# First mixer of a three-layer block on one core: heads one after another, division folded into the norm

## The chip, the cores and the metric

The kernel runs on one core of a Trainium2 chip, as one launch. The metric is the device time in microseconds (us). TensorE is called PE, VectorE DVE, ScalarE ACT, GpSimd POOL, SyncE SP, as in the profile.

## The reference, cut to what matters

Three layers with residual stream `x` of 512 tokens by 1024 features, fp32. The first layer's mixer is an mLSTM with 4 heads (keys 128 wide, values 256 wide). Per chunk it computes:

```python
d = jnp.exp(log_d - m_t[..., None])
s = jnp.einsum('bhtd,bhsd->bhts', qb, kb) * d
...
den = jnp.sum(s, axis=-1) + inter * jnp.einsum('bhd,bhtd->bht', n, qb)
h_out = num / jnp.maximum(jnp.abs(den), jnp.exp(-m_t))[..., None]
...
hs = rms_norm(hs, head_gain.reshape(H, dv))
og = jax.nn.sigmoid(o.astype(jnp.float32)).reshape(B, S, H, dv)
out = (hs * og).reshape(B, S, D_MODEL).astype(h.dtype)
return out @ w_out
```

After it come a residual add with a norm, cross-attention into 256 memory tokens, a feed-forward part, and two more layers, which the change leaves alone.

## The kernel before

Features lie on the partitions and the 512 tokens along the free dimension. The kernel computes the chunked recurrence as one causal attention over all 512 tokens: per head a score matrix in four blocks of 512, 384, 256 and 128 columns (1280 in all, offsets `AT`), times a decay matrix `ml_w`. Weights come from memory in units of 128x1024 (8 tiles of 128x128): SP loads a unit into one of 2 landing buffers, ACT writes its upper half `w_hi` (L777, `hi_to`), POOL the rest `w_lo` (L1731, `lo_to`), both into a ring of 4. A tile of a projection is three matmuls (`tile`, L359): upper by upper, upper weights by lower activations, lower weights by upper activations; so an output of 8 tiles is 24 matmuls of 512 columns. The mixer's inner products (scores, sums, values) are plain fp32 matmuls. A unit's ring place comes free when PE has multiplied it (`unit_done`). All five engines run their own list of instructions in order, tied by semaphores; `await_empty` makes PE wait until a PSUM bank was read out.

Order of the first mixer: projections q, k, the gates, the output gate `ml_og` (DVE L1228, ACT sigmoid), then the values `ml_v` by token (`by_token`, L416: two groups of four units, banks 0 to 3, then 4 to 7). Then PE spreads two rows per head over all partitions (L457), one for the decays (`M_bc`, copied by DVE L1311), one for the denominator's floor (`floor_bc`, ACT L890), and turns `uT` (L461). DVE computes the decays' arguments (L1323), ACT their exponentials (L895).

Then the heads go in two pairs. For a pair: both heads' scores (PE L470), both heads' weights and causal mask (DVE L1331, L1335), then for each head the sum over the weights (denominator, 1280 columns) and two value products (numerator, 2560 columns; both PE L481). ACT takes the denominator's absolute value (L901), DVE its maximum with the floor (L1343), its reciprocal (L1345) and the product with the numerator out of PSUM (L1350). ACT squares the result (L905), PE sums the squares over partitions (L492, L493), ACT computes the reciprocal root (L907, L909); POOL multiplies by the output gate (L1778) meanwhile. DVE applies root (L1357) and gain (L1359), ACT writes the upper half `u_hi` (L913), DVE the lower half `u_lo` (L1363). The second pair's arguments and weights begin on DVE after the first pair's `u_lo`. The projection `ml_out` (L359) waits for all eight `u_lo` tiles, then makes its 8 outputs one after another; ACT copies each out (L821), DVE sums squares (L1250, L1252), and the memory's norm is computed beside it (L928, L1372).

Of the kernel before, what the change touches and what calls it, by code (L numbers as in the profile page):

```python
# [14 lines left out]
P = 128  # L15
# [135 lines left out]
def build(nc, units, xT, memT, vecs_d, gates_w, gates_b, pool_w, conv_d, consts_d, masks_d, out):  # L151
    assert units.shape[0] == UNITS
    ctx = ExitStack()
    with ctx:
# [109 lines left out]
        for name, size in (("e0", 1024), ("e1", 1024), ("a0", 1024), ("a1", 1024), ("sc", 1024), ("state", 512),  # L264
# [27 lines left out]
        ml_og_at, ml_arg, ml_exp, ml_s, ml_den, ml_h_at, ml_sq, ml_r, ml_gated, ml_scaled = (  # L292
            sem(n) for n in ("ml_og", "ml_args", "ml_decays", "ml_weights", "ml_den", "ml_h", "ml_h_squared", "ml_h_rstd", "ml_h_gated", "ml_h_scaled"))
# [48 lines left out]
        def tensor_engine():  # L342
# [92 lines left out]
            def mlstm():  # L435
# [13 lines left out]
                by_token("ml_v", u_tok, 4)  # L449
                for h in range(ML_H):  # L450
                    sel = sel_all[0:4, h * P:(h + 1) * P]
                    b = 2 * (h % 2)
                    for bank, row in ((b, w1), (b + 1, w2)):
                        if h == 0:
                            pe.wait_ge(*(ml_gate_v.at(7) if bank == 0 else ml_gate_s.at(7)))
                        await_empty([bank])
                        pe.matmul(ps[:, bank, :], sel, row, start=True, stop=True).then_inc(*full[bank].up())  # L457
                        holds(("ml_bc", h, bank % 2), [bank], full[bank].now())
                await_empty([0])
                for b in range(4):  # L460
                    ins = pe.transpose(ps[:, 0, 4 * b:4 * b + 4], rows[0:4, 0, b * P:(b + 1) * P], ident[0:4, 0:4])  # L461
                ins.then_inc(*full[0].up())
                holds("ml_uT", [0], full[0].now())
                for i in range(2):
                    for j in range(2):
                        h, B0 = 2 * i + j, 3 * j
                        await_empty([B0, B0 + 1, B0 + 2])
                        for b in range(4):
                            a0 = 512 * B0 + AT[b]
                            ins = pe.matmul(flat[:, a0:a0 + S - b * P], ml_kT[:, h, b * P:(b + 1) * P], ml_qT[:, h, b * P:S],  # L470
                                            start=b != 3, stop=b != 1, skip_group_check=True)
                        ins.then_inc(*full[B0].up())
                        holds(("ml_s", h), [B0, B0 + 1, B0 + 2], full[B0].now())
                    for j in range(2):
                        h, B0 = 2 * i + j, 3 * j
                        for n in range(3):
                            if n == 0:
                                pe.wait_ge(*ml_s.at(h + 1))
                            for b in range(4):
                                lhs = ones if n == 0 else ml_v[:, b, h * ML_DV + (n - 1) * P:h * ML_DV + n * P]  # L480
                                ins = pe.matmul(ps[:, B0 + n, b * P:S], lhs, ml_w[:, j, AT[b]:AT[b] + S - b * P],  # L481
                                                start=b == 0, stop=b == 3, skip_group_check=True)
                            if n == 0:
                                ins.then_inc(*full[B0].up())
                                holds(("ml_den", h), [B0], full[B0].now())
                        ins.then_inc(*full[B0 + 1].up())
                        holds(("ml_num", h), [B0 + 1, B0 + 2], full[B0 + 1].now())
                    for j in range(2):
                        h = 2 * i + j
                        pe.wait_ge(*ml_sq.at(h + 1))  # L490
                        await_empty([6 + j])
                        pe.matmul(ps[:, 6 + j, :], ones, sq[:, 0, 0:S], start=True, stop=False)  # L492
                        pe.matmul(ps[:, 6 + j, :], ones, sq[:, 1, 0:S], start=False, stop=True).then_inc(*full[6 + j].up())  # L493
                        holds(("ml_ss", h), [6 + j], full[6 + j].now())
                pe.wait_ge(*o_lo_at.at(8))
                outputs("ml_out", SQUARE, u_rhs, ONE, four)
# [270 lines left out]
        def scalar_engine():  # L767
# [65 lines left out]
            def mlstm():  # L833
# [35 lines left out]
                table("natural_log_exp_and_others")  # L869
                for j in range(8):  # L870
# [6 lines left out]
                    if j == 1:  # L877
                        act.wait_ge(*ml_gate_s.now())
                        act.activation(w1, w1, ACT.Ln, bias=1.0).then_inc(*ml_gate_s.up())
                    if j % 4 == 3:  # L880
# [4 lines left out]
                    if j == 4:  # L885
                        act.wait_ge(*ml_gate_v.at(9))
                        act.activation(w2, w2, ACT.Exp, scale=-1.0).then_inc(*ml_gate_s.up())
                for h in range(ML_H):
                    act.wait_ge(*ready_at["ml_bc", h, 1])
                    act.activation(floor_bc[:, h, :], ps[:, banks_at["ml_bc", h, 1][0], :], ACT.Copy).then_inc(*emptied_by["ml_bc", h, 1])  # L890
                for i in range(2):
                    for j in range(2):
                        h = 2 * i + j
                        act.wait_ge(*ml_arg.at(h + 1))
                        act.activation(ml_w[:, j, :], ml_w[:, j, :], ACT.Exp, scale=-1.0).then_inc(*ml_exp.up())  # L895
                    for j in range(2):
                        h, B0 = 2 * i + j, 3 * j
                        act.wait_ge(*ready_at["ml_den", h])
                        if i:
                            act.wait_ge(*o_lo_at.at(2 * h - 2))  # L900
# [5 lines left out]
                        act.wait_ge(*ready_at["ml_ss", h])  # L906
# [287 lines left out]
        def vector_engine():  # L1194
            def own():

                dve.wait_ge(*dve_own.now())
# [714 lines left out]
```

## Time and profile before

| | |
|---|---|
| time, 3 runs | median 2699.49 us (2697.83 to 2703.25) |
| profiled execution: its time | 2702.27 us |
| its span | 2700.9 us |
| PE matmul busy | 2456.8 us (91%) |
| DVE / ACT / POOL busy | 982.2 / 897.1 / 1064.4 us |
| mean granted TensorE clock | 0.951 |

Times in views are us from the start of the span. A matmul's end is modelled, so consecutive matmuls overlap in the list; the chain of waits gives better durations for a run of them. A granted clock of 1.00 is 2.4 GHz, 0.50 is 1.2 GHz.

### The profile page before, as it was taken

To read this page: it belongs to the slowest core of one execution; us is meant where nothing else is said; L and a number is where in the kernel's file an instruction comes from. 1 tells how busy PE (TensorE), PEld (TensorE's weight loads), DVE (VectorE), ACT (ScalarE), POOL (GpSimd) and SP (SyncE) were. 2 spreads that over 40 slices of the span, in tenths; PEclk is the share of its full clock that TensorE was granted. 3 is DMA by queue.
4 is the path that set the end of the run, shared out by engine and by line. 5 is a ranking of instruction groups with operands and counts; after the bars stand their busy time and mean duration, and the time that the engine had idled before them with its cause. 6 is when DMAs were issued, how large, how long until landed. Compare 5 with 4: busy or idle time off the path is not lost.

```text
span 2700.9 us, 29218 instructions
## 1 busy us (share of the span) xinstructions
PE 2456.8 (91%) x12268; PEld 2017.8 (75%) x12268; DVE 982.2 (36%) x1312; ACT 897.1 (33%) x1194; POOL 1064.4 (39%) x466
## 2 busy tenths in 40 slices
PE   7986898899999798989888999997998998899997
PEld 5754775678888586668666788885988998799885
DVE  3245623422211411444423422204556442754402
ACT  4322432332222323664323322223434323322221
POOL 5321551444444442005514444444423433444442
PEclk9987998899999898999899999998989999999998
DMA  4211230122233121003312222222200222132231
GB/s 146 86 39 34 99 125 24 56 101 97 98 101 102 63 94 55 1 1 102 125 39 70 71 94 97 99 102 85 87 32 27 99 79 79 63 99 91 92 109 70
DMA packets 62850, 211.47 MB, mean 78 GB/s; under 512 B 8704, under 2 KB 10880, under 8 KB 62720
## 3 DMA queue, kind: packets, MB, share of 16 engines
q1 hardware_dynamic: 57968, 206.20, 22.8%
q10 hardware_dynamic: 4752, 3.42, 0.4%
q8 instruction: 97, 1.59, 0.2%
q14 instruction: 33, 0.27, 0.0%
HBM read 207.49 MB, written 2.10 MB: 78 GB/s over the span
## 4 chain that ended last, share of the span: by engine, by line
PE 80%; DVE 12%; ACT 4%; issue 2%; DMA 1%; POOL 0%; ACTq 0%; SPq 0%; DVEq 0%
PE ps L359 64%; PE ps L416 4%; DVE x L1212 3%; DVE u_lo L1203 2%; DVE arena L1210 2%; PE ps L544 1%; PE ps L611 1%; PE ps L651 1%; PE ps L524 1%; PE ps L481 1%; DVE y_ffn L1210 1%; PE ps L597 1%; PE ps L587 1%; PE ps L599 1%; DMA w_land<-in_units 1%
## 5 line engine op out<-in xcount | busy, mean ns | idle before, releaser
L1731 POOL TENSOR_TENSOR w_lo<-w_land,w_hi 128x1024 fp32r<-128x1024 f32 x384 | 955.1, 2489 | 1398.6 <-ACT w_hi L777 1398.2
L359 PE MATMUL ps<-u_hi,w_hi 128*128 128x512 f32 (+2 forms) x2448 | 800.1, 358 | 99.5 <-DVE u_lo L1203 62.6
L359 PE MATMUL ps<-u_lo,w_hi 128*128 128x512 f32 (+2 forms) x2448 | 797.1, 357 | 0.0
L359 PE MATMUL ps<-u_hi,w_lo 128*128 128x512 f32 (+2 forms) x2448 | 792.8, 355 | 0.0
L359 PEld LDWEIGHTS ps<-u_hi,w_hi 128*128 128x128 f32 x2448 | 437.5, 191 | 188.5 <-issue 51.5
L777 ACT ACTIVATE w_hi<-w_land 128x1024 fp32r<-128x1024 f32 x384 | 403.2, 1051 | 478.8 <-PE ps L359 350.4
L359 PEld LDWEIGHTS ps<-u_hi,w_lo 128*128 128x128 f32 x2448 | 435.3, 191 | 66.4
L359 PEld LDWEIGHTS ps<-u_lo,w_hi 128*128 128x128 f32 x2448 | 434.9, 191 | 66.0 <-issue 0.7
L359 PE MATMUL ps<-hid_hi,w_lo 128*128 128x512 f32 x528 | 208.3, 395 | 0.0
L359 PE MATMUL ps<-hid_lo,w_hi 128*128 128x512 f32 x528 | 208.3, 395 | 0.0
L359 PE MATMUL ps<-hid_hi,w_hi 128*128 128x512 f32 x528 | 208.3, 395 | 0.0
L1250 DVE TENSOR_TENSOR sq<-y_ffn 128x512 f32<-128x512 f32 x24 | 16.6, 692 | 329.7 <-ACT y_ffn L821 329.7
L1228 DVE TENSOR_TENSOR arena<-ps,rstd 128x264 f32<-128x264 f32 (+1 forms) x92 | 46.0, 530 | 247.0 <-PE ps L359 230.2
L1463 DVE TENSOR_TENSOR arena<-ps,rstd 128x512 f32<-128x512 f32 x66 | 45.6, 690 | 239.3 <-PE ps L359 239.3
L999 ACT ACTIVATE hid_hi<-arena 128x512 fp32r<-128x512 f32 x66 | 41.7, 631 | 246.6 <-DVE arena L1466 246.6
L359 PEld LDWEIGHTS ps<-hid_hi,w_lo 128*128 128x128 f32 x528 | 99.5, 188 | 23.3
L359 PEld LDWEIGHTS ps<-hid_hi,w_hi 128*128 128x128 f32 x528 | 99.5, 188 | 23.2
L359 PEld LDWEIGHTS ps<-hid_lo,w_hi 128*128 128x128 f32 x528 | 99.5, 188 | 23.1
L1740 POOL TENSOR_TENSOR acc<-acc,sq 128x512 f32<-128x512 f32 (+1 forms) x42 | 66.0, 1571 | 57.5 <-ACT sq L800 56.6
L1250 DVE TENSOR_TENSOR sq<-arena 128x512 f32<-128x512 f32 (+1 forms) x40 | 27.8, 695 | 163.4 <-ACT arena L821 163.4
L796 ACT ACTIVATE u_hi<-x,vecs 128x512 fp32r<-128x512 f32 (+1 forms) x64 | 46.3, 723 | 120.5 <-DVE x L1212 120.5
L821 ACT ACTIVATE arena<-ps 128x512 f32<-128x512 f32 (+1 forms) x48 | 24.5, 529 | 160.2 <-PE ps L359 160.2
(281 smaller groups left out, 2930.0 us busy)
## 6 DMA issues: line engine op xcount, KB each, us to landing
w_land<-in_units SPq DMA_DIRECT2D x384, 512.0 KB, 3.2
x<-in_xT SPq DMA_DIRECT2D x4, 528.0 KB, 7.1
arena<-in_memT ACTq DMA_DIRECT2D x2, 1024.0 KB, 5.2
outT<-x SPq DMA_DIRECT2D x8, 256.0 KB, 2.0
consts<-in_consts SPq DMA_DIRECT2D x1, 448.0 KB, 7.8
arena<-in_masks ACTq DMA_DIRECT2D x1, 448.0 KB, 3.4
arena<-in_consts ACTq DMA_DIRECT2D x1, 296.0 KB, 3.8
arena<-in_consts ACTq DMA_DIRECT2D x1, 256.0 KB
```

The costliest lines, as they stand in the source:

```text
L359: ins = pe.matmul(ps[:, bank, 0:c1 - c0], w, rhs(k, c0, c1)[which], start=first and h == 0, stop=last and h == 2)
L416: ins = pe.matmul(ps[:, 4 * g + b, :], a_, w_[:, u % RING, cols], start=k == 0 and n == 0, stop=k == DT - 1 and n == 2)
L777: act.activation(w_hi[:, u % RING, :], w_land[:, u % LAND, :], ACT.Copy).then_inc(*unit_hi.up())
L796: act.activation(u_hi[:, k, a:z], x[:, k, a:z], ACT.Copy, scale=col(gain, k)).then_inc(*u_hi_at.up())
L1203: dve.scalar_tensor_tensor(u_lo[:, k, a:z], x[:, k, a:z], col(gain, k), u_hi[:, k, a:z].bitcast(F32), ALU.mult, ALU.subtract).then_inc(*u_ ...
L1210: dve.scalar_tensor_tensor(y[:, k, :], y[:, k, :], col(POST[p], k), rstd_y[:, cols], ALU.mult, ALU.mult).then_inc(*dve_own.up())
L1212: dve.tensor_tensor(x[:, k, cols], x[:, k, cols], y[:, k, :], ALU.add).then_inc(*x_new.up())
L1228: ins = dve.tensor_tensor(v, p_, rstd[:, c0:c1], ALU.mult)
L1250: dve.tensor_tensor(sq[:, o % 2, 0:w], y[:, o, :], y[:, o, :], ALU.mult).then_inc(*dve_own.up())
L1463: dve.tensor_tensor(w, bank, rs, ALU.mult).then_inc(*emptied_by[name, o])
L1731: pool.tensor_tensor(w_lo[:, u % RING, :], w_land[:, u % LAND, :], w_hi[:, u % RING, :].bitcast(F32), ALU.subtract).then_inc(*unit_lo.up())
L1740: pool.tensor_tensor(acc[:, a:z], acc[:, a:z], sq[:, k % 2, a:z], ALU.add).then_inc(*x_sum.up())
```

## The change

- The heads go one by one. The next head's scores are issued behind this head's denominator and ahead of the previous head's sum of squares and this head's numerator. Each engine's list is rewritten to match: while head h's weights, denominator and numerator are made, head h-1 is normed.
- The spreading of the rows (8 matmuls and `uT`) moves between units 5 and 6 of `ml_v`; the copies, the arguments and the exponentials of heads 0 and 1 move with it on DVE and ACT. The ACT copies of the floor become squares.
- Division folded into the norm: ACT squares denominator and numerator straight out of PSUM (scaled by eps for the denominator); DVE adds the floored square to the mean square; ACT's reciprocal root of that serves for both. Reciprocal, product and absolute value go.
- The output gate is multiplied by DVE out of PSUM; POOL's four gate products go. Root and gain are one instruction per tile.
- `ml_out` begins its first three outputs abreast, tile by tile as each `u_lo` comes; the other five follow as before.

```diff
-    by_token("ml_v", u_tok, 4)
...
+    def broadcasts():
+
+        for h in range(ML_H):
...
+                pe.matmul(ps[:, bank, :], sel, row, start=True, stop=True).then_inc(*full[bank].up())
...
+    by_token("ml_v", u_tok, 4, [(5, broadcasts)])
...
+    def weighted(h, n, lhs):
+        B0 = 3 * (h % 2)
...
+            ins = pe.matmul(ps[:, B0 + n, b * P:S], lhs(b), ml_w[:, h % 2, AT[b]:AT[b] + S - b * P],
...
+    def denominator(h):
+        B0 = 3 * (h % 2)
+        pe.wait_ge(*ml_s.at(h + 1))
+        weighted(h, 0, lambda b: ones).then_inc(*full[B0].up())
...
+    def numerator(h):
+        B0 = 3 * (h % 2)
+        for n in range(2):
+            ins = weighted(h, n + 1, lambda b: ml_v[:, b, h * ML_DV + n * P:h * ML_DV + (n + 1) * P])
+        ins.then_inc(*full[B0 + 1].up())
...
+    def square_sum(h):
+        bank = 6 + h % 2
+        pe.wait_ge(*ml_sq.at(h + 1))
+        await_empty([bank])
+        pe.matmul(ps[:, bank, :], ones, sq[:, 0, 0:S], start=True, stop=False)
+        pe.matmul(ps[:, bank, :], ones, sq[:, 1, 0:S], start=False, stop=True).then_inc(*full[bank].up())
...
+    scores(0)
+    scores(1)
     for h in range(ML_H):
...
-            ins.then_inc(*full[B0].up())
...
-                    pe.wait_ge(*ml_s.at(h + 1))
...
-                    ins = pe.matmul(ps[:, B0 + n, b * P:S], lhs, ml_w[:, j, AT[b]:AT[b] + S - b * P],
...
-            pe.wait_ge(*ml_sq.at(h + 1))
...
-            pe.matmul(ps[:, 6 + j, :], ones, sq[:, 0, 0:S], start=True, stop=False)
-            pe.matmul(ps[:, 6 + j, :], ones, sq[:, 1, 0:S], start=False, stop=True).then_inc(*full[6 + j].up())
...
-    pe.wait_ge(*o_lo_at.at(8))
-    outputs("ml_out", SQUARE, u_rhs, ONE, four)
+        denominator(h)
+        if 1 <= h < ML_H - 1:
+            scores(h + 1)
+        if h:
+            square_sum(h - 1)
+        numerator(h)
+    square_sum(ML_H - 1)
+
+    for o in range(3):
+        await_empty(four(o))
+    for k in range(UT):
+        pe.wait_ge(*o_lo_at.at(k + 1))
+        for o in range(3):
+            ins = tile(UNIT["ml_out"] + o, k, k, u_rhs, ONE, four(o), k == 0, k == UT - 1)
+            if k == UT - 1:
+                ins.then_inc(*unit_done.up())
+                holds(("ml_out", o), four(o), unit_done.at(UNIT["ml_out"] + o + 1))
+    outputs("ml_out", SQUARE, u_rhs, ONE, four, 3)
...
+        if j == 6:
+            for h in range(ML_H):
+                act.wait_ge(*ready_at["ml_bc", h, 1])
+                act.activation(floor_bc[:, h, :], ps[:, banks_at["ml_bc", h, 1][0], :], ACT.Square, scale=EPS ** 0.5).then_inc(*emptied_by["ml_bc", h, 1])
+            decays(0)
+            decays(1)
...
+    def denominator_square(h):
+
...
+        if h >= 2:
+            act.wait_ge(*ml_scaled.at(2 * h - 2))
+        act.activation(d, ps[:, 3 * (h % 2), :], ACT.Square, scale=EPS ** 0.5).then_inc(*emptied_by["ml_den", h])
...
+    def numerator_square(h):
+        act.wait_ge(*ready_at["ml_num", h])
+        if h:
+            act.wait_ge(*ready_at["ml_ss", h - 1])
+        act.activation(sq[:, :, 0:S], ps[:, 3 * (h % 2) + 1:3 * (h % 2) + 3, :], ACT.Square).then_inc(*ml_sq.up())
...
+    def rstd_head(h):
+        d = den[h % 2]
+        act.wait_ge(*emptied_at["ml_ss", h])
+        act.activation(d, d, ACT.Ln).then_inc(*act_own.up())
+        act.wait_ge(*act_own.now())
+        act.activation(d, d, ACT.Exp, scale=-0.5).then_inc(*ml_r.up())
...
+    def uppers(h):
+        for n in range(2):
+            kk = 2 * h + n
+            act.wait_ge(*ml_scaled.at(kk + 1))
+            act.activation(u_hi[:, kk, XS], ml_h[:, 2 * (h % 2) + n, :], ACT.Copy).then_inc(*o_hi_at.up())
...
     for h in range(ML_H):
...
-            act.activation(den[j], ps[:, B0, :], ACT.Abs).then_inc(*emptied_by["ml_den", h])
-            act.wait_ge(*emptied_at["ml_num", h])
-            if h:
-                act.wait_ge(*ready_at["ml_ss", h - 1])
-            act.activation(sq[:, :, 0:S], ml_h[:, 2 * j:2 * j + 2, :], ACT.Square).then_inc(*ml_sq.up())
...
-            act.activation(den[j], ps[:, 6 + j, :], ACT.Ln, bias=eps[:, 0:1], scale=1.0 / ML_DV).then_inc(*emptied_by["ml_ss", h])
-            act.wait_ge(*emptied_at["ml_ss", h])
-            act.activation(den[j], den[j], ACT.Exp, scale=-0.5).then_inc(*ml_r.up())
...
+        denominator_square(h)
+        if h:
+            rstd_head(h - 1)
+            uppers(h - 1)
+        numerator_square(h)
+        if h + 2 < ML_H:
+            decays(h + 2)
+    rstd_head(ML_H - 1)
+    uppers(ML_H - 1)
...
+        if j == 6:
+            for h in range(ML_H):
+                dve.wait_ge(*ready_at["ml_bc", h, 0])
+                dve.tensor_copy(M_bc[:, h, :], ps[:, banks_at["ml_bc", h, 0][0], :]).then_inc(*emptied_by["ml_bc", h, 0])
+            dve.wait_ge(*ready_at["ml_uT"])
...
+            arguments(0)
+            arguments(1)
...
+    def weights(h):
...
+        dve.tensor_tensor(w, flat[:, 512 * 3 * (h % 2):512 * 3 * (h % 2) + SPAN], w, ALU.mult).then_inc(*emptied_by["ml_s", h])
...
+    def floor(h):
...
+        dve.tensor_tensor(den[h % 2], den[h % 2], floor_bc[:, h, :], ALU.max).then_inc(*dve_own.up())
+
+    def gated(h):
+        B0, n = 3 * (h % 2), 2 * (h % 2)
+        dve.wait_ge(*ready_at["ml_num", h])
...
+        dve.wait_ge(*ml_sq.at(h + 1))
...
+        dve.tensor_tensor(ml_h[:, n:n + 2, :], ps[:, B0 + 1:B0 + 3, :], ml_og[:, 2 * h:2 * h + 2, :], ALU.mult).then_inc(*emptied_by["ml_num", h])
+
+    def mean_square(h):
...
+        dve.wait_ge(*ready_at["ml_ss", h])
...
+        dve.scalar_tensor_tensor(d, ps[:, 6 + h % 2, :], 1.0 / ML_DV, d, ALU.mult, ALU.add).then_inc(*emptied_by["ml_ss", h])
+
+    def normed(h):
+        dve.wait_ge(*ml_r.at(h + 1))
...
+        for n in range(2):
+            h_ = ml_h[:, 2 * (h % 2) + n, :]
+            dve.scalar_tensor_tensor(h_, h_, col("ml_head", 2 * h + n), den[h % 2], ALU.mult, ALU.mult).then_inc(*ml_scaled.up())
...
+    weights(0)
+    weights(1)
     for h in range(ML_H):
...
-            dve.tensor_tensor(den[j], den[j], floor_bc[:, h, :], ALU.max).then_inc(*dve_own.up())
...
-            dve.reciprocal(den[j], den[j]).then_inc(*dve_own.up())
...
-            dve.tensor_tensor(h_, ps[:, B0 + 1:B0 + 3, :], one(den[j]).broadcast_to([P, 2, S]), ALU.mult).then_inc(*emptied_by["ml_num", h])
...
-                dve.tensor_tensor(h_, h_, one(den[n // 2]).broadcast_to([P, 2, S]), ALU.mult).then_inc(*dve_own.up())
...
-            dve.tensor_scalar(ml_h[:, n, :], ml_h[:, n, :], col("ml_head", kk), None, ALU.mult).then_inc(*ml_scaled.up())
...
+        floor(h)
+        if 1 <= h < ML_H - 1:
+            weights(h + 1)
+        if h:
+            mean_square(h - 1)
+            normed(h - 1)
+            lowers(h - 1)
+        gated(h)
+        if h + 2 < ML_H:
+            arguments(h + 2)
+    mean_square(ML_H - 1)
+    normed(ML_H - 1)
+    lowers(ML_H - 1)
...
-pool.wait_ge(*ml_og_at.at(8))
-for h in range(ML_H):
-    j = h % 2
-    h_ = ml_h[:, 2 * j:2 * j + 2, :]
-    pool.wait_ge(*ml_sq.at(h + 1))
-    pool.tensor_tensor(h_, h_, ml_og[:, 2 * h:2 * h + 2, :], ALU.mult).then_inc(*ml_gated.up())
```

## Rows read from the trace of the kernel before

**Rows 1.** The profile's page: busy shares, and the chain's shares by engine.

```profile
PE 2456.8 (91%) x12268; PEld 2017.8 (75%) x12268; DVE 982.2 (36%) x1312; ACT 897.1 (33%) x1194; POOL 1064.4 (39%) x466
...
PE 80%; DVE 12%; ACT 4%; issue 2%; DMA 1%; POOL 0%; ACTq 0%; SPq 0%; DVEq 0%
```

**Rows 2.** Windows: length, busy time (instructions) by engine, granted clock, DMA share, GB/s.

```profile
160.40:169.90 9.50, 9.26 (x21) 3.93 (x20) 4.26 (x7) 3.58 (x6) 0.00 (x0) 0.77 0.08 32
177.20:192.10 14.90, 14.88 (x54) 8.80 (x52) 7.66 (x8) 1.65 (x2) 2.35 (x1) 1.00 0.00 0
192.10:200.50 8.40, 0.04 (x1) 0.04 (x1) 6.41 (x5) 2.86 (x4) 0.01 (x1) 0.74 0.00 0
209.70:216.30 6.60, 0.01 (x2) 0.01 (x1) 6.57 (x15) 2.54 (x2) 0.00 (x0) 0.77 0.00 0
233.10:241.50 8.40, 0.03 (x1) 0.03 (x1) 6.41 (x5) 2.86 (x4) 0.00 (x1) 0.74 0.00 0
241.50:251.30 9.80, 3.78 (x5) 1.17 (x5) 7.55 (x10) 3.51 (x6) 2.34 (x1) 0.50 0.00 0
```

**Rows 3.** The chain of waits from 100 to 300: start, length, what.

```profile
115.88 44.53 PE ps L416 x192
160.41 8.92 PE ps L457 x16
...
177.35 13.01 PE ps L481 x48
190.36 0.86 PE ps L492 x2
...
235.72 3.36 DVE rstd_y L1345
...
251.27 40.53 PE ps L359 x168
```

**Rows 4.** A window over a stretch in which the granted clock stood at 0.50.

```profile
165.46:175.70 10.24, 9.97 (x19) 4.91 (x18) 5.85 (x12) 3.73 (x4) 0.00 (x0) 0.50 0.00 0
```

**Rows 5.** Groups by line, 160.4 to 251.3: busy us, mean ns | idle before, releaser.

```profile
L1323 DVE SCALAR_TENSOR_TENSOR arena<-arena,uT,zrow 128x512 f32<-128x512 f32 (+3 forms) x16 | 7.6, 545 | 0.0
...
L1331 DVE TENSOR_TENSOR arena<-ps,arena 128x1280 f32<-128x1280 f32 x4 | 5.9, 1487 | 1.3 <-PE ps L470 1.3
...
L895 ACT ACTIVATE arena<-arena 128x1280 f32<-128x1280 f32 x4 | 5.1, 1270 | 6.6 <-DVE arena L1323 6.6
...
L913 ACT ACTIVATE u_hi<-arena 128x512 fp32r<-128x512 f32 x8 | 4.6, 617 | 1.5 <-DVE arena L1359 1.5
L905 ACT ACTIVATE sq<-arena 128x1024 f32<-128x1024 f32 x4 | 4.2, 1057 | 21.6 <-DVE arena L1350 21.6
L1335 DVE TENSOR_TENSOR arena<-arena,consts 128x128 f32<-128x128 f32 x16 | 3.6, 285 | 0.1
...
L1357 DVE TENSOR_TENSOR arena<-arena,rstd_y 128x1024 f32<-128x1024 f32 x2 | 2.5, 1225 | 4.3 <-ACT rstd_y L909 4.3
L1350 DVE TENSOR_TENSOR arena<-ps,acc 128x1024 f32<-128x1024 f32 x2 | 2.4, 1224 | 0.1
...
L1343 DVE TENSOR_TENSOR rstd_y<-rstd_y,arena 128x512 f32<-128x512 f32 x2 | 1.4, 692 | 16.8 <-ACT rstd_y L901 16.8
L907 ACT ACTIVATE acc<-ps,eps 128x512 f32<-128x512 f32 x2 | 1.4, 687 | 10.9 <-PE ps L493 10.9
...
L909 ACT ACTIVATE rstd_y<-rstd_y 128x512 f32<-128x512 f32 x2 | 1.3, 630 | 0.1
```

**Rows 6.** Timeline of DVE, 306 to 330: a two-factor product of 512 columns.

```profile
308.54 0.74 DVE L1210 SCALAR_TENSOR_TENSOR arena<-arena,vecs,rstd_y 128x512 f32<-128x512 f32 x1
```

**Rows 7.** Timeline of ACT, 251 to 310: the third output's copy.

```profile
269.58 0.60 ACT L821 ACTIVATE arena<-ps 128x512 f32<-128x512 f32 x1 [4.01 <-PE ps L359]
```

**Rows 8.** The page's groups: the making of a unit's two halves.

```profile
L1731 POOL TENSOR_TENSOR w_lo<-w_land,w_hi 128x1024 fp32r<-128x1024 f32 x384 | 955.1, 2489 | 1398.6 <-ACT w_hi L777 1398.2
...
L777 ACT ACTIVATE w_hi<-w_land 128x1024 fp32r<-128x1024 f32 x384 | 403.2, 1051 | 478.8 <-PE ps L359 350.4
```

More of the change, by code:

```diff
@@ L448, in mlstm @@
                 outputs("ml_og", SQUARE, u_rhs, ONE, four)
-                by_token("ml_v", u_tok, 4)
-                for h in range(ML_H):
[L451 to L458, printed above, removed]
@@ L495, in mlstm @@
-                pe.wait_ge(*o_lo_at.at(8))
-                outputs("ml_out", SQUARE, u_rhs, ONE, four)
+                def broadcasts():
+                    for h in range(ML_H):
+                        sel = sel_all[0:4, h * P:(h + 1) * P]
+                        b = 2 * (h % 2)
+                        for bank, row in ((b, w1), (b + 1, w2)):
+                            if h == 0:
+                                pe.wait_ge(*(ml_gate_v.at(7) if bank == 0 else ml_gate_s.at(7)))
+                            await_empty([bank])
+                            pe.matmul(ps[:, bank, :], sel, row, start=True, stop=True).then_inc(*full[bank].up())
+                            holds(("ml_bc", h, bank % 2), [bank], full[bank].now())
+                    await_empty([0])
+                    for b in range(4):
+                        ins = pe.transpose(ps[:, 0, 4 * b:4 * b + 4], rows[0:4, 0, b * P:(b + 1) * P], ident[0:4, 0:4])
+                    ins.then_inc(*full[0].up())
+                    holds("ml_uT", [0], full[0].now())
@@ new lines, in mlstm, with scores @@
+                by_token("ml_v", u_tok, 4, [(5, broadcasts)])
+                def scores(h):
+                    B0 = 3 * (h % 2)
+                    await_empty([B0, B0 + 1, B0 + 2])
+                    for b in range(4):
+                        a0 = 512 * B0 + AT[b]
+                        ins = pe.matmul(flat[:, a0:a0 + S - b * P], ml_kT[:, h, b * P:(b + 1) * P], ml_qT[:, h, b * P:S],
+                                        start=b != 3, stop=b != 1, skip_group_check=True)
+                    ins.then_inc(*full[B0].up())
+                    holds(("ml_s", h), [B0, B0 + 1, B0 + 2], full[B0].now())
@@ new lines, in weighted @@
+                def weighted(h, n, lhs):
+                    B0 = 3 * (h % 2)
+                    for b in range(4):
+                        ins = pe.matmul(ps[:, B0 + n, b * P:S], lhs(b), ml_w[:, h % 2, AT[b]:AT[b] + S - b * P],
+                                        start=b == 0, stop=b == 3, skip_group_check=True)
+                    return ins
+                def denominator(h):
+                    B0 = 3 * (h % 2)
+                    pe.wait_ge(*ml_s.at(h + 1))
+                    weighted(h, 0, lambda b: ones).then_inc(*full[B0].up())
+                    holds(("ml_den", h), [B0], full[B0].now())
@@ L869, in mlstm, with decays @@
                 table("natural_log_exp_and_others")
+                def decays(h):
+                    act.wait_ge(*ml_arg.at(h + 1))
+                    act.activation(ml_w[:, h % 2, :], ml_w[:, h % 2, :], ACT.Exp, scale=-1.0).then_inc(*ml_exp.up())
                 for j in range(8):
@@ L879, in mlstm @@
                         act.activation(w1, w1, ACT.Ln, bias=1.0).then_inc(*ml_gate_s.up())
+                    if j == 4:
+                        act.wait_ge(*ml_gate_v.at(9))
+                        act.activation(w2, w2, ACT.Exp, scale=-1.0).then_inc(*ml_gate_s.up())
+                    if j == 6:
[4 more added lines that the diff above has]
+                        decays(1)
                     if j % 4 == 3:
@@ new lines, in rstd_head @@
+                def rstd_head(h):
+                    d = den[h % 2]
+                    act.wait_ge(*emptied_at["ml_ss", h])
[7 more added lines that the diff above has]
+                        act.activation(u_hi[:, kk, XS], ml_h[:, 2 * (h % 2) + n, :], ACT.Copy).then_inc(*o_hi_at.up())
```

140 lines of the change are left out of this document (39 added, 101 removed).

## Prediction

> **What bounds the kernel now.** I read the page first. PE is busy for 91% of the span and makes up 80% of the chain that ended last, DVE 12%, ACT 4% [rows 1]. So PE sets the time, and what can be won is time in which PE stands still or runs slowly. The page's average says nothing of the stretch that the change touches, so I cut that stretch into windows between the events of the chain. Here the reader sees the picture turn: PE is fully busy from 177.2 to 192.1, then has no work at all for 8.4 us, again for 6.6 us (209.7 to 216.3), again for 8.4 us (233.1 to 241.5), and from 241.5 to 251.3 works 3.78 of 9.8 us [rows 2]. That is 29.4 us of PE idle between the first denominator (177.35) and `ml_out` (251.27). In the gaps DVE is the busy one, and the chain of waits names its reciprocal with 3.36 us, one in each of the two 8.4 us gaps [rows 3]. The granted clock also falls: it stands at 0.50 in the last window of rows 2, and around the row spreading of L457 it is at 1.2 GHz for 10.24 us with PE busy for 9.97 of it, which is 5.1 us of work lost [rows 4].
>
> **Up to the first denominator.** A unit of `ml_v` takes 44.53/8 = 5.57 us, so unit 5 ends at 115.88 + 6 x 5.57 = 149.3 [rows 3]. Now the spreading comes in there: 8 matmuls at 0.86 (the price of one 512-column fp32 matmul, L492 in rows 3) and some 0.2 for `uT`, 7.1 us at 2.4 GHz. Then units 6 and 7, 11.1 us. The clock fell during the spreading before, which had full-rate work ahead of it as it has now, so I carry the loss of 5.1 us over [rows 4]; its bounds are nothing (no fall) and 7 us. `ml_v` ends at 149.3 + 7.1 + 11.1 + 5.1 = 172.6. What moves along costs nothing while this cover stands: copies, arguments (1.90 us per head, 7.6/4) and exponentials (1.27 us) of heads 0 and 1 [rows 5] are done by about 165 on idle engines, with some 8 us to spare. Queued behind ACT's wait for the arguments is the upper half of the third `ml_out` unit, wanted only 50 us later, and behind DVE's the value copies, which PE wants from the numerator on. Without the cover it would be the 4 to 5 us between spreading and scores that they cost before.
>
> Then head 0's scores. A head's 1280 columns take 13.01/6 = 2.17 us [rows 3]: 174.8. DVE's weights take 1.49 + 0.90 (3.6/4, mask) [rows 5], with 0.2 us from PE's last matmul to the consumer: 177.4. Before, the denominator began at 177.35 [rows 3]. So this move alone earns nothing: PE does the same work in another order, and loses the same to the clock.
>
> **The heads.** Denominator and numerator of head 0 are 3 x 2.17 = 6.5 us: 183.9. ACT squares the numerator (1.06, L905's price), DVE gates it (1.22, L1350's): 186.5. From there to the next head's gating a chain runs between DVE and ACT; in order, with the nearest row for each [rows 5, 6]: next but one head's arguments 1.90; exponentials 1.27; square of the denominator 0.60 (a 512-column ACT read of PSUM, rows 7); floor 0.69; weights 1.49 + 0.90; mean square 0.69 (as the floor; at most 0.74); Ln 0.69; Exp 0.63; two normed tiles 2 x 0.74; second upper half 0.62; square of the numerator 1.06; gating 1.22. That is 13.24, and 13.6 with twelve hand-overs of 0.03 us. PE's work in such a period is scores 2.17, denominator 2.17, sum of squares 1.72, numerator 4.34, together 10.4; it waits about 3.2 us for PSUM banks 3 to 5, which the gating empties. So DVE and ACT set the pace of the heads. Two periods: gating of head 2 ends at 213.7, having begun at 212.4.
>
> From 212.4 PE sets it again: sum of squares of head 2 1.72, numerator of head 3 4.34, 0.2, its square 1.06, its sum of squares 1.72, hand-overs 0.1: 221.5. Check by PE's account. Its work from 177.4 is 4 x 6.5 + 2 x 2.17 + 4 x 1.72 = 37.2 us in both kernels. Before, 73.9 us passed: 37.2 work, 29.4 idle, 7.3 lost to the clock. After, 44.1 us: 37.2 and 6.9 idle. The gain is 22.5 us of idle time and 7.3 us of clock.
>
> Operations with no row: squares out of two PSUM banks cost 1.06 (from SBUF) to 1.20 (two reads of 0.60), four on the path, so up to 0.6 us more; a gain is excluded, as no read here was cheaper by the column. The gating reads PSUM beside SBUF; rows show 1224 ns for that and 1225 ns with both factors in SBUF [rows 5], so no difference. The Trainium skill, VectorE: DVE Perf Modes, The TRN2 errata, gives a PSUM source 62 more cycles than an SBUF source; as an estimate that would be 65 ns a gating, 0.3 us in all. The trace does not agree, and the row stands.
>
> POOL's four products (L1778) vanish. Nothing on the path waited for them except in the order of DVE's scaling, and POOL is idle around them, so 0 us of their own; that DVE no longer meets POOL there is inside the prices above, which are those of quiet stretches.
>
> **`ml_out`.** PE has the tiles of heads 0 to 2 when it arrives at 221.5. Six tiles for three outputs are 12.5 us of work; the last tile needs 0.2 + 0.69 + 0.69 + 0.63 + 1.48 + 0.62 + 0.69 = 5.0 us after the last sum of squares, so it is hidden. Three outputs take 3 x 5.57 = 16.7 us: 238.2. The clock is at 2.4 GHz here if the waits before it are as short as worked out. Before, the third output was copied at 269.58 [rows 7], hence done at 269.4. After this the order is the old one. Three ring places come free almost together; the next unit but one needs a copy 0.60, upper half 1.05, lower half 2.49 [rows 7, 8], 4.1 us, beside a unit of 5.57. The cover is 1.4 us; if it were gone, each unit would be late by the excess. The memory's load is issued 17 us before the fourth output wants it.
>
> **The sum.** 269.4 - 238.2 = 31.2 us less. The profiled execution took 2702.3, 2.8 above the median of the runs; 2702.3 - 31.2 = 2671.1, by the median 2668.3.
>
> **Rivals.** (A) This forecast, 2664 to 2671 (small terms above, and falls of the clock in later stages landing elsewhere by a few us): 0.56.
>
> (B) The clock falls again in a 3.2 us wait between the heads. For: it fell within each gap of 6.6 us and more. Against: by the mean clocks 0.74 and 0.77 of those windows it was low for the last 4.4 of 8.4 us and the last 3.0 of 6.6 us, so it fell 3.6 to 4.0 us into them, later than a wait of 3.2 us lasts [rows 2]. One fall as long as in rows 4 costs at most 5.1 us, less what the wait absorbs: 2 to 5 us a fall, one or two falls, 2670 to 2678. Chance 0.25.
>
> (C) The spreading, being split from the scores by two dense units, costs little clock: up to 5 us more gain, 2660 to 2664. Chance 0.09.
>
> (D) The overlap fails: a wait, say of DVE in `normed` in front of the next gating, strings the heads up one by one and only reciprocals and products out of the way count. Two reciprocals and their products in the two gaps, 2 x (3.36 + 1.22) = 9.2 us: about 2690. Against: each order was followed above. Chance 0.06.
>
> (E) Slower: the clock goes down at the spreading and stays down, since PE now has a short wait in every head instead of a few long ones. PE's work from 156.4 to `ml_out` is 11.1 + 8.7 + 26.0 + 6.9 = 52.7 us; at 1.2 GHz 105.4, and three outputs 33.4: 295.2, 26 us later than before, 2725. It decides from some 62 us of low clock beyond the forecast. For it: low stretches outlast their cause by several us [rows 4]. Against: 2.4 GHz came back before 177 while PE ran the same kind of matmul. Chance 0.04. The Trainium skill, TensorE: Matmul & The Clock Gate, A second HAM failure mode, reports this kind of swing from small stops between groups of matmuls; by that rule B and E are the cases to fear, and no row of this trace shows it for stops this short.
>
> **How the numbers follow.** The likeliest case gives 2668. C and the later stages reach down to 2661, B up to 2676; D, E and the far end of B stay outside, about 1.5 in 10. What this kernel's measurement can tell from no change is about 0.2%, 5.4 us; A to D, 0.96, are faster by more; I leave 0.01 of it for no change and say faster 0.95, same 0.01, slower 0.04.
>
> **What would show it.** In the profile after: L1345, L1357, L1778 gone; `ml_v` ends near 172.6 and the first denominator starts near 177.4; gatings of heads 0, 1, 2 are 13.6 us apart, with PE stops of 3.2 us before the scores of head 3; the last sum of squares ends near 221.5 at granted clock 1.00; the third output is copied near 238. The prediction is wrong if DVE's or ACT's order adds a wait to the period, if the clock reads 0.50 between 180 and 221, or if PE waits for w_lo behind the third output.

## The result, and the profile after

The changed kernel takes 2674.94 us (median of 4 runs, 2673.47 to 2676.97) against 2701.37 us before on the same chip (4 runs, 2697.83 to 2703.28): ratio 0.9904 [0.9887, 0.9921], 26.4 us less. The forecast was 2668, its range 2661 to 2676. The profiled execution took 2673.47 us beside the 2702.27 us of before, 28.8 less where the sum said 31.2. Its mean granted clock is 0.960 (before 0.951).

The page's busy shares and chain by engine, after (before: [rows 1]):

```profile
PE 2446.1 (92%) x12268; PEld 2008.9 (75%) x12268; DVE 979.4 (37%) x1308; ACT 896.9 (34%) x1194; POOL 1055.9 (40%) x462
...
PE 77%; DVE 14%; ACT 5%; issue 2%; DMA 1%; POOL 1%; ACTq 0%; SPq 0%; DVEq 0%
```

PE issues the same 12268 matmuls, busy for 10.7 us less: that is clock. About half of it, 5.0 us, lies behind the first mixer, in stages that the change leaves alone. The rest of the gain is idle time. The chain of waits after, to be read against [rows 3]:

```profile
150.05 11.14 PE ps L459 x16
161.19 0.33 PE ps L463 x4
161.51 13.58 PE ps L416 x48
175.09 2.17 PE ps L474 x8
...
179.84 6.75 PE ps L482 x24
...
221.03 1.12 PE ps L503 x2
222.16 0.86 PE ps L504 x2
223.01 15.31 PE ps L359 x66
```

From the first denominator (179.84) to `ml_out` (223.01) is 43.2 us, where before it was 73.9. Windows over the same stretch, columns as in [rows 2]:

```profile
150.10:161.20 11.10, 11.10 (x19) 4.33 (x19) 2.77 (x4) 2.85 (x4) 2.34 (x1) 0.62 0.20 70
161.20:175.10 13.90, 13.90 (x52) 11.25 (x53) 3.96 (x9) 4.20 (x4) 2.39 (x1) 0.81 0.06 17
...
179.80:188.90 9.10, 8.90 (x32) 5.53 (x32) 4.15 (x8) 1.62 (x2) 0.00 (x0) 1.00 0.00 0
188.90:201.90 13.00, 10.59 (x36) 6.29 (x36) 9.46 (x18) 5.19 (x7) 0.00 (x0) 1.00 0.00 0
201.90:214.90 13.00, 11.87 (x39) 6.96 (x40) 9.46 (x18) 5.67 (x8) 0.00 (x0) 1.00 0.01 1
214.90:223.00 8.10, 6.99 (x23) 3.90 (x22) 5.27 (x7) 3.54 (x5) 0.00 (x0) 1.00 0.00 0
```

Here the reader sees both halves of the gain. The heads hold 4.85 us of idle PE (0.20 + 2.41 + 1.13 + 1.11) where [rows 2] had 29.4, and the clock reads 1.00 throughout. But in the first two windows, the row spreading and the two units behind it, PE is never idle and still runs at 0.62 and 0.81.

What became of the gain is read by marks, before against after: third output done 269.4 / 239.8 (29.6 us earlier); keys of the memory begin 298.23 / 270.37 (27.9); first scaling of `y`, the mixer's output, 305.43 / 278.24 (27.2, called **the mark** below, and in the expectations "DVE's first addition to x"); end of the span 2700.9 / 2672.2 (28.7). So 2.4 us are lost again between the third output and the mark, and 1.5 come back later: behind the mark PE is busy for 5.0 us less and idle for 3.6 us more. DVE's timeline after the third output shows the loss:

```profile
238.97 0.69 DVE L1304 TENSOR_TENSOR sq<-arena 128x512 f32<-128x512 f32 x1 [10.51 <-ACT arena L852]
239.70 0.69 DVE L1306 TENSOR_TENSOR acc<-acc,sq 128x512 f32<-128x512 f32 x1
240.48 2.73 DVE L1304 TENSOR_TENSOR sq<-arena 128x512 f32<-128x512 f32 x1
243.25 2.79 DVE L1306 TENSOR_TENSOR acc<-acc,sq 128x512 f32<-128x512 f32 x1
246.07 0.69 DVE L1304 TENSOR_TENSOR sq<-arena 128x512 f32<-128x512 f32 x1
```

and POOL's in the same microseconds, with PE's first matmul on the memory's keys:

```profile
239.97 5.51 POOL L1812 TENSOR_TENSOR w_lo<-w_land,w_hi 128x1024 fp32r<-128x1024 f32 x2 [7.99 <-ACT w_hi L808]
```

```profile
270.37 0.39 PE L359 MATMUL ps<-m_hi,w_hi 128*128 128x256 f32 x1 [2.44 <-DVE m_lo L1453]
```

The outputs that finish together hand DVE their sums in one bunch, while POOL makes two `w_lo` in one go. A sum that takes 0.69 us alone takes 2.73 and 2.79 when it begins while POOL's `w_lo` runs, DVE falls behind, and PE waits 2.44 us for `m_lo`, the lower half of the normed memory; before, that wait was 0.44. From the third output to the keys the chain of waits is DVE's alone; before, it was PE's there (L359 in [rows 3]) but for the last 6.4 us:

```profile
240.48 2.75 DVE sq L1304
...
243.25 2.80 DVE acc L1306
...
251.48 2.52 DVE m_lo L1453
...
265.47 2.82 DVE sq L1304
...
270.31 2.81 DVE sq L1304
```
The Trainium skill, SBUF — State Buffer, Who interferes with whom, says that a DVE instruction with two SBUF inputs contends with a GpSimd instruction that reads SBUF, and calls the contention an exclusive lock. DVE's and POOL's rows agree: the two slow sums take about as long as one `w_lo` (two in 5.51 us), while the sum at 239.70, begun 0.27 us ahead of POOL, takes 0.69. It is POOL that is then held up: in the kernel before, a `w_lo` that began 0.27 us behind such a sum took 2.69 us, where one that met no sum took 2.38.

### The profile page after: what moved, and what is told of

The parts are those of the page before. It is cut to its first block, busy times and chain, and to the rows that moved or that the text cites. A ratio compares the mean times of both kernels' runs of the same rounds, so it can differ in the third digit from the quotient of the medians.

```text
span 2672.2 us, 29212 instructions
## 1 busy us (share of the span) xinstructions
PE 2446.1 (92%) x12268; PEld 2008.9 (75%) x12268; DVE 979.4 (37%) x1308; ACT 896.9 (34%) x1194; POOL 1055.9 (40%) x462
## 4 chain that ended last, share of the span: by engine, by line
PE 77%; DVE 14%; ACT 5%; issue 2%; DMA 1%; POOL 1%; ACTq 0%; SPq 0%; DVEq 0%
PE ps L359 63%; PE ps L416 4%; DVE x L1266 3%; DVE u_lo L1257 2%; DVE arena L1264 2%; PE ps L575 1%; PE ps L642 1%; PE ps L555 1%; DVE y_ffn L1264 1%; DMA w_land<-in_units 1%; PE ps L618 1%; PE ps L682 1%; DVE sq L1304 1%; PE ps L628 1%; POOL w_lo L1812 1%
## 5 line engine op out<-in xcount | busy, mean ns | idle before, releaser
L359 PE MATMUL ps<-u_hi,w_hi 128*128 128x512 f32 (+2 forms) x2448 | 800.3, 358 | 95.6 <-DVE u_lo L1257 63.9
L359 PE MATMUL ps<-u_lo,w_hi 128*128 128x512 f32 (+2 forms) x2448 | 796.9, 357 | 0.0
L359 PE MATMUL ps<-u_hi,w_lo 128*128 128x512 f32 (+2 forms) x2448 | 793.4, 355 | 0.0
L359 PEld LDWEIGHTS ps<-u_hi,w_hi 128*128 128x128 f32 x2448 | 438.0, 191 | 183.7 <-issue 53.5
L359 PEld LDWEIGHTS ps<-u_hi,w_lo 128*128 128x128 f32 x2448 | 435.5, 191 | 66.1
L359 PEld LDWEIGHTS ps<-u_lo,w_hi 128*128 128x128 f32 x2448 | 435.4, 191 | 66.1 <-issue 1.0
L359 PE MATMUL ps<-hid_hi,w_lo 128*128 128x512 f32 x528 | 208.3, 395 | 0.0
L359 PE MATMUL ps<-hid_lo,w_hi 128*128 128x512 f32 x528 | 208.3, 395 | 0.0
L359 PE MATMUL ps<-hid_hi,w_hi 128*128 128x512 f32 x528 | 208.3, 394 | 0.0
L1544 DVE TENSOR_TENSOR arena<-ps,rstd 128x512 f32<-128x512 f32 x66 | 45.6, 691 | 239.8 <-PE ps L359 239.8
L359 PEld LDWEIGHTS ps<-hid_hi,w_hi 128*128 128x128 f32 x528 | 99.5, 188 | 23.4
L359 PEld LDWEIGHTS ps<-hid_hi,w_lo 128*128 128x128 f32 x528 | 99.5, 188 | 23.3
L359 PEld LDWEIGHTS ps<-hid_lo,w_hi 128*128 128x128 f32 x528 | 99.5, 188 | 23.0
L1304 DVE TENSOR_TENSOR sq<-arena 128x512 f32<-128x512 f32 (+1 forms) x40 | 37.4, 934 | 147.8 <-ACT arena L852 147.6
L1528 DVE TENSOR_TENSOR arena<-ps,rstd 128x512 f32<-128x512 f32 x44 | 30.4, 691 | 126.4 <-PE ps L359 104.6
```

The costliest lines, as they stand in the source:

```text
L359: ins = pe.matmul(ps[:, bank, 0:c1 - c0], w, rhs(k, c0, c1)[which], start=first and h == 0, stop=last and h == 2)
L1304: dve.tensor_tensor(sq[:, o % 2, 0:w], y[:, o, :], y[:, o, :], ALU.mult).then_inc(*dve_own.up())
L1544: dve.tensor_tensor(w, bank, rs, ALU.mult).then_inc(*emptied_by[name, o])
```

## The experiments

Each median is of 4 runs (6 for pairs_folded and order_alone). The mark is read from each profile; it resolves what the median cannot, since the time from the mark to the end of the span differed from profile to profile by up to 8.7 us (2390.8 to 2399.5) though nothing is changed there, and by 3.5 us between the three profiles of the changed kernel.

| label | median, us | ratio to before [95%] | mark, us |
|---|---|---|---|
| after_again | 2674.27 | 0.9886 [0.9869, 0.9902] | 278.38 |
| one_by_one | 2669.96 | 0.9865 [0.9850, 0.9880] | 273.76 |
| spread_late | 2671.99 | 0.9871 [0.9856, 0.9885] | 279.00 |
| spread_split | 2674.29 | 0.9882 [0.9867, 0.9897] | 275.90 |
| pairs_folded | 2693.67 | 0.9968 [0.9955, 0.9981] | 298.15 |
| order_alone | 2681.44 | 0.9923 [0.9909, 0.9937] | 288.14 |
| rows128 | 2669.05 | 0.9880 [0.9864, 0.9895] | 273.68 |
| split3_one | 2665.48 | 0.9870 [0.9856, 0.9884] | 273.70 |
| after_base | 2674.73 | 0.9905 [0.9884, 0.9927] | 278.45 |
| rows128_one | 2665.49 | 0.9870 [0.9850, 0.9889] | 271.45 |
| square_first | 2663.33 | 0.9857 [0.9836, 0.9878] | 268.58 |

Before stood at 2706.24 beside the first four, 2701.14 beside the next four, 2701.11 beside the last three; each of these three batches ran on another chip.

### The changed kernel again

> The changed kernel once more, as the base on the same chip for the three below: about 2675 us, 26 below the kernel before. Both theories expect the same: spreading at 1.2 GHz for 10 to 14 us, gatings about 13 us apart, PE 2.4 us idle before the keys of the memory.

> The changed kernel as the base on the same chip for the two below: 2673 to 2676 us, DVE's first addition to x near 278.5.

2674.27 and 2674.73 us: the same kernel, twice more. The PE stop of 2.44 us before the keys is there both times, and in none of the three profiles does the clock fall between the heads. The kernel before moved by 5 us from one batch to another, so differences to it are 26 to 32 us; kernels of one batch are compared with each other. The middle batch has no run of the changed kernel, so its four are compared with it by the marks and by the time before.

### Outputs one by one again

```diff
-for o in range(3):
-    await_empty(four(o))
-for k in range(UT):
-    pe.wait_ge(*o_lo_at.at(k + 1))
-    for o in range(3):
...
-outputs("ml_out", SQUARE, u_rhs, ONE, four, 3)
+output("ml_out", 0, SQUARE, u_rhs, ONE, four(0), {k: o_lo_at.at(k + 1) for k in range(UT)})
+outputs("ml_out", SQUARE, u_rhs, ONE, four, 1)
```

> Only edit: ml_out makes its first output alone, waiting tile by tile for the lower halves, instead of three abreast. Theory (the bunching costs): DVE's sums for the outputs no longer fall beside POOL's making of w_lo, PE's stop before the memory's keys goes back from 2.4 to about 0.4 us, the sum of y is ready about 0.7 us earlier, and the first output loses 0.8 us waiting for its last tiles: 1.5 to 2.5 us faster than three abreast. Rival (three abreast is worth its cover): the last tiles come 5 us after the last sum of squares and one output has only 4.1 us of work before them, so PE waits and the time is 1 us or more slower.

4.3 us faster than after_again, more than the 1.5 to 2.5 expected; the mark is 4.6 us earlier. DVE's sums of the third output, with 4.03 us of rest ahead of them, and PE's stop before the keys:

```profile
238.62 0.69 DVE L1296 TENSOR_TENSOR sq<-arena 128x512 f32<-128x512 f32 x1 [4.03 <-ACT arena L844]
239.34 0.69 DVE L1298 TENSOR_TENSOR acc<-acc,sq 128x512 f32<-128x512 f32 x1
```

```profile
266.56 0.39 PE L359 MATMUL ps<-m_hi,w_hi 128*128 128x256 f32 x1 [0.44 <-DVE m_lo L1445]
```

The bunch is gone and so is the stop; DVE still meets POOL in the first output's sums (2.52 and 2.77 us), but has caught up by the third. The last sum of squares ended 2.3 us earlier than in after_again (220.81 for 223.11), ahead of the edit and no effect of it: in this execution `ml_v` began 1.2 us earlier and the low clock of the spreading was shorter (10.2 us for 13.7), so `ml_v` ended at 172.43, though the clock fell again at head 3's scores:

```profile
199.40 3.78 PE L474 MATMUL ps<-arena 128*128 128x512 f32 x8 [2.38 <-DVE arena L1400]
```

The same scores take 2.39 us in the changed kernel. The other 2.3 us of the mark lie behind the last sum of squares and are the edit's, 2.0 of them the stop. The other profiles repeat it: from the last sum of squares to the mark it is 55.1 to 55.3 us in the six profiles of head-by-head kernels with three outputs abreast and the division folded, and 53.0 us in one_by_one, split3_one and rows128_one. So taking the outputs abreast costs here, and earns nothing.

### Where the spreading stands

Spread_late puts it back behind the eight units of `ml_v`; spread_split issues it a head at a time behind units 4 to 7; split3_one in three pieces, with the outputs one by one.

```diff
-by_token("ml_v", u_tok, 4, [(5, broadcasts)])
+by_token("ml_v", u_tok, 4)                                                        # spread_late
+broadcasts()
...
+by_token("ml_v", u_tok, 4, [(4 + h, lambda h=h: spread(h)) for h in range(ML_H)])  # spread_split
+by_token("ml_v", u_tok, 4, [(4, lambda: spread(0)), (5, lambda: spread(1)), (6, lambda: (spread(2), spread(3)))])  # split3_one
```

> Only edit: the spreading of the rows is back behind the last unit of the values, with its copies, arguments and exponentials. Theory (the place of the spreading earns nothing): arguments and exponentials of head 0 come back onto the path (2 to 4 us), the clock's loss may shrink from 6.9 to about 5 us; within 3 us of three abreast with the early place. Rival (the early place hides real work): 4 us or more slower.

> Only edit: one head's two row matmuls behind each of the last four units of the values (uT behind the first) instead of all eight behind one. Theory (a long run of 4-row matmuls brings the clock down): runs of 1.7 us leave the clock at 1.00 through the values, which end near 168 instead of 175, and the time falls by 5 to 7 us. Rival (any such matmul counts against the clock, in pieces too): the clock still reads 0.50 for 10 us or more in 145 to 175 and the time stays within 2 us.

> Both repairs together: rows of head 0 spread behind the fifth unit of the values, of head 1 behind the sixth, of heads 2 and 3 behind the seventh; ml_out one output at a time. Theory (both losses are separate and add up): DVE's first addition to x comes 7 to 9 us before that of the changed kernel (278.5), and the time is 6 to 10 us lower, 2665 to 2668. Rival (what the first mixer gives the clock takes back later): the stage is earlier by that much, but the time is no lower than with one output at a time alone.

Spread_late: the first denominator starts at 180.63 (after: 179.84) and the mark moves by 0.6 us; the median is 2.3 us lower than after_again's, against the mark. The clock is low for the same 13.7 us. The move is worth nearly nothing. Spread_split: a pair of matmuls takes 1.91 us, the clock is low for 3.4 us instead of 13.7, and `ml_v` ends at 170.34; but head 0's scores wait for the last row's copy until 172.52, the mark comes only 2.5 us earlier, and the total shows nothing of it. That miss of the expected 5 to 7 us is in part the new wait (2.2 us) and in part low clock in later stages: behind the mark PE is busy for 8.0 us more than in after_again, with the same matmuls. Split3_one ends `ml_v` at 172.34 with two low stretches of 3.4 us there; its mark is where one_by_one's is, 4.7 us ahead of the changed kernel's where 7 to 9 were expected, so that the two gains add up is not shown by it, though its time (2665 to 2668 expected) came.

### Rows of 128 for the spreading

The same sixteen matmul records, but with all 128 rows of weights and of the operand, the added ones zero.

```diff
-sel = sel_all[0:4, h * P:(h + 1) * P]
-for bank, row in ((b, w1), (b + 1, w2)):
+sel = sel_all[:, h * P:(h + 1) * P]
+for bank, row in ((b, rows[:, 2, 0:S]), (b + 1, rows[:, 3, 0:S])):
...
+dve.memset(rows[:, 2:4, 0:S], 0.0)
```

> The changed kernel, but the spreading's eight matmuls use all 128 rows (rows 4 to 127 are zero) instead of 4. Theory (what lowers the clock is how little of the array the 4-row matmuls use): the clock stays at 1.00 through the spreading, which takes 7 us instead of 11, and the values end near 168. Rival (the form of the instruction or the zero data counts, not the rows): the clock falls as before and the time stays within 2 us.

> 128-row spreading and one output at a time together. Theory (separate losses, adding up): values end near 170, DVE's first addition to x near 269 to 271, time 2662 to 2666, 9 to 12 below the changed kernel. Rival (both gains are mostly where the clock's falls land further on): no better than either alone, 2668 to 2670.

Groups by line around the spreading, first of the changed kernel, then of rows128_one (busy us, mean ns):

```profile
L459 PE MATMUL ps<-arena 4*128 4x512 f32 x16 | 11.2, 871 | 0.0
```

```profile
L459 PE MATMUL ps<-arena 128*128 128x512 f32 x16 | 7.0, 592 | 0.0
```

The same window of the changed kernel and of rows128:

```profile
151.80:158.70 6.90, 6.90 (x11) 2.79 (x10) 1.42 (x3) 1.79 (x3) 1.82 (x1) 0.58 0.23 76
```

```profile
151.80:158.70 6.90, 6.90 (x18) 2.79 (x17) 2.77 (x4) 2.85 (x4) 2.35 (x1) 1.00 0.32 118
```

With PE busy without a break in both, the clock reads 0.58 in one and 1.00 in the other, and the chain gives the spreading 6.87 us instead of 11.14. The two units behind it take 11.27 instead of 13.58: 6.6 us in all. That decides between the explanations of the low clock: it comes with the 4-row form, and neither the place of the spreading nor a gap is needed for it. The other profiles agree: the clock falls at the spreading in all ten with 4 rows, and in none of the three with 128 (rows128, rows128_one, square_first).

Of the 6.6 us `ml_v`'s end (170.30, expected near 168) shows 4.8, since unit 5 ended 1.8 us later. Part of that is the edit's own price. Its memset stands on the chain of waits, and PE's first long stop, 2.21 to 2.48 us in the three profiles of the changed kernel, is longer behind it:

```profile
24.21 0.91 DVE L1317 MEMSET arena<- 128x1024 f32 x1 [0.16 <-issue]
```

```profile
31.70 0.50 PE L359 MATMUL ps<-u_hi,w_hi 128*128 128x512 f32 x1 [3.17 <-POOL w_lo L1813]
```

With the pause ahead of it the memset adds 1.1 us to the chain; this execution had been 0.5 us ahead. The other 1.2 us go with low clock behind the stop, 0.79 from 32 to 40 for 1.00 in the changed kernel's first profile. Whether the longer stop caused it stays open, since after_again (0.87) and after_base (0.90) have it without a memset. Rows128_one (outputs one by one too) is 9.2 us faster than after_base, within its expectation, its mark 2.2 us earlier than rows128's.

### The folded division without the order, and the order without it

Pairs_folded is the kernel before, heads in pairs, with the division folded, the gate from PSUM and one instruction for root and gain. Order_alone is the changed kernel with absolute value, reciprocal, product and bias in the logarithm put back; both products are DVE's.

```diff
-act.activation(den[j], ps[:, B0, :], ACT.Abs)
+act.activation(den[j], ps[:, B0, :], ACT.Square, scale=EPS ** 0.5)
...
-dve.reciprocal(den[j], den[j]).then_inc(*dve_own.up())
...
+dve.scalar_tensor_tensor(den[j], ps[:, 6 + j, :], 1.0 / ML_DV, den[j], ALU.mult, ALU.add)
```

> The kernel before with the arithmetic of the changed one alone: heads still in pairs, spreading and ml_out as before, but squares straight from PSUM, the floored square added to the mean square, gating by DVE from PSUM, no reciprocal. Theory (the order earns most): each 8.4 us stop of PE between a pair's two sums of squares shrinks to about 4 us and the clock falls less often, 9 to 16 us faster than before (some 2690), so the order is worth the other half or more. Rival (the arithmetic earns nearly all): 20 us or more faster than before.

> The changed kernel with the arithmetic of the kernel before: head by head, early spreading, three abreast, but absolute value, reciprocal, product, square of the product, reciprocal root straight from PSUM; gating by DVE in SBUF. Theory (DVE and ACT set the pace of the heads): reciprocal and second product lengthen a head's period from 13.0 to 15 to 16 us, 7 to 12 us slower than the changed kernel. Rival (PE sets the pace): as the changed kernel within 3 us.

Pairs_folded is only 7.5 us faster than before, where 9 to 16 were expected: the idle time between a pair's sums of squares shrank from 8.4 to about 3.5 us, but the clock was still low behind it. Its chain, with two matmuls that cost 0.86 at 2.4 GHz:

```profile
228.59 0.86 PE ps L492 x2
229.45 0.87 PE ps L493 x2
...
233.81 1.78 PE ps L492 x2
235.59 1.72 PE ps L493 x2
```

Order_alone is 19.7 us faster than before. In its chain DVE gates the heads (here it divides them) at 187.81, 201.69 and 215.57, a period of 13.9 us:

```profile
184.42 3.37 DVE acc L1401
187.81 0.04 DVE arena L1407
...
201.69 1.22 DVE arena L1407
...
215.57 1.23 DVE arena L1407
...
231.97 15.41 PE ps L359 x66
```

The period was expected at 15 to 16: with reciprocal and product in it, it is only 0.9 us longer than the changed kernel's 13.0, so most of the reciprocal's 3.35 us lies in time in which the chain waited for others. The last head has no such cover. From the product of head 2 (215.57) to `ml_out` (231.97) it is 16.4 us, 7.1 more than from the gating of head 2 in the changed kernel (213.67 to 223.01), and the reciprocal is on the chain again:

```profile
219.77 3.37 DVE rstd_y L1401
```

The clock was low there too, for 3.4 us from 218.4, behind a PE stop of 2.52 us, and for as long once more from 228.6. So the folded division earns more at the end of the heads than in their period: order_alone's mark is 9.9 us behind the changed kernel's, inside the 7 to 12 expected. The two parts add up: 7.5 + 19.7 = 27.2, the whole is 26.4 (26 to 32 in other batches); by the marks it is 7.3 + 17.3 = 24.6, the whole 27.2. "Order" means here the place of the spreading (worth nearly nothing) and the outputs abreast (2.3 us lost) as well.

### A better version

Square_first is rows128_one with ACT squaring the numerator ahead of the previous head's upper halves, and DVE gating ahead of its lower halves.

```diff
     rstd_head(h - 1)
-    uppers(h - 1)
-numerator_square(h)
+numerator_square(h)
+if h:
+    uppers(h - 1)
...
     normed(h - 1)
-    lowers(h - 1)
 gated(h)
 if h + 2 < ML_H:
     arguments(h + 2)
+if h:
+    lowers(h - 1)
```

> The kernel above, and in each head ACT squares the numerator ahead of the previous head's two upper halves, DVE gates and computes the next arguments ahead of its lower halves. Theory (the DVE-ACT chain sets the pace of the heads): the two upper halves and their hand-overs leave the chain, a period shrinks from 13.0 to about 11.4 us, PE's stop before scores from 2.4 to about 1 us, 3 to 5 us faster than the kernel above. Rival (the chain is bound elsewhere, or the lower halves delay weights as much as they gain): within 1 us of it.

2663.33 us, 38 less than before and 11 less than the changed kernel. Its chain:

```profile
182.98 1.22 DVE arena L1402
...
194.19 1.23 DVE arena L1402
195.42 0.14 issue
195.55 2.40 PE ps L474 x8
```

The gatings are 11.2 us apart instead of 13.0, near PE's own 10.4, PE's stop before head 3's scores is 0.61 us instead of 2.38, and the mark is 2.9 us earlier than rows128_one's. The median is 2.2 lower, less than the 3 to 5 expected, with ranges that overlap (2658.62 to 2666.44, 2664.14 to 2669.89), so the step from rows128_one is shown by the profile and not by the time.

## Why the prediction was right

- **The mechanism held.** The heads' idle time went, with the clock that it had cost: 73.9 us became 43.2, forecast 44.1. Order_alone, with 19.7 of the 26 us, shows that the order alone earns most of it; rival D (the overlap fails) is out, and its 9.2 us for reciprocals and products is near the 7.5 that pairs_folded shows they are worth alone. That POOL's four products were worth nothing of their own was not tested apart.
- **"This move alone earns nothing."** Right: spread_late has its mark 0.6 us from the changed kernel's.
- **The clock's loss at the spreading, 5.1 us, was too small.** It was low for 13.7 us, 6.9 us of work, the end of its bounds (0 to 7). With unit 5's end 0.75 us later than worked out (150.05), `ml_v` ended at 175.09 instead of 172.6. I took the loss over from [rows 4] as a property of the place; rows128 shows that it belongs to the 4-row matmuls. Rival C's lower loss is had by giving them 128 rows, and in one execution by splitting them up (spread_split, 3.4 us of low clock), not by moving them as one run.
- **The period of 13.6 us was 13.0.** The DVE gatings:

```profile
187.73 1.22 DVE L1408 TENSOR_TENSOR arena<-ps,arena 128x1024 f32<-128x1024 f32 x1 [4.11 <-ACT sq L943]
200.69 1.23 DVE L1408 TENSOR_TENSOR arena<-ps,arena 128x1024 f32<-128x1024 f32 x1 [0.29 <-ACT sq L943]
213.67 1.23 DVE L1408 TENSOR_TENSOR arena<-ps,arena 128x1024 f32<-128x1024 f32 x1 [0.29 <-ACT sq L943]
```

  The chain of the period was the one followed in the prediction. Where one instruction starts before the end of its neighbour, less than its whole length is on the path (the floor 0.57 of its 0.69 us, the denominator's square 0.50 of 0.59), and that covers the hand-overs that were added. PE stopped 2.4 us before head 3's scores, forecast 3.2. The gating's price was right, 1225 ns. The square of two PSUM banks takes 1014 ns, below the 1.06 us given as its lower bound: the gain that the prediction excluded is there, 0.04 us each.
- **"After this the order is the old one."** This step failed. I followed the ring of `w_lo` behind the bunched outputs, which had its cover, and not DVE's sums of the same outputs, which met POOL. It lost 2.4 us, 2.0 of them as PE's stop before the keys; one_by_one takes that away. The third output was done at 239.8, but ACT copied it only at 241.21, behind two upper halves, where the forecast had 238. The sign that I gave for this, a wait for `w_lo`, did not come, though the loss did.
- **Rivals B and E.** E did not come. B did not come in the changed kernel's profiles, but it did in one_by_one, rows128 and split3_one: the clock was low for 3.4 us from about the start of head 3's scores. PE lost 1.6 to 1.7 us each time, and the waits behind absorbed all but 0.3 to 0.5 of it, below the 2 to 5 that I gave a fall. The ground on which B was held unlikely, that the clock falls only 3.6 us into a wait, does not hold: here it fell 2.1 to 3.2 us after PE had stopped. What decides between the two outcomes in stops of the same 2.4 us stays open.

The account: 31.2 forecast; less 2.5 (`ml_v` later), plus 0.9 (heads), gives the 29.6 at the third output; less 2.4 up to the mark; plus 1.5 in the stages behind gives 28.7. The last term lies inside the 8.7 us by which those stages differ between the profiles, and has no cause that I could show. That it gave back more than half of the 2.4 is luck, and the measured 2674.94 stands only 1.1 us inside the range. So the forecast came in range with two terms off in its disfavour, the clock at the spreading and the bunched outputs, and one in its favour, the period.

## What to carry to other kernels

When an order is changed so that results come in a bunch, follow every engine that takes them, not only the one that makes the next operands. When the clock is low while TensorE has no gap, look at the shape of its matmuls: filling unused rows with zeros gave back 6.6 us here, less 1.1 us for a memset that stood on the chain; issued later it might cost nothing, which no run tried. And where a chain between two engines sets the pace, put the instruction that frees PSUM ahead of everything that is wanted later.

## What the runs showed of the hardware

- Sixteen fp32 matmul records with 4 rows, no idle time between them: clock down to 1.2 GHz, 11.14 us. With 128 rows: 2.4 GHz throughout, 6.87 us.
- A DVE product or sum of two SBUF operands (512 columns) takes 0.69 us, and up to 2.88 when it begins while POOL's `w_lo` runs (2.73 and 2.79 above, 2.52 and 2.77 in one_by_one). Begun 0.27 us ahead of POOL it takes 0.69, and POOL's 2.69 instead of 2.38.
- Of the nine profiles with a PE stop of 2.38 us before head 3's scores, three (one_by_one, rows128, split3_one) ran the next 3.4 us at 1.2 GHz and six did not; behind order_alone's stop of 2.52 us the clock was low as well, and behind square_first's stop of 0.61 us it was not.
- ACT squares 1024 columns in 1014 ns out of PSUM and in 1057 ns out of SBUF; DVE's product of 1024 columns takes 1224 to 1225 ns with one operand in PSUM or none.
